# Splitting the next linear's input inside the last chunk of the linear before it, in a 256-token, three-block Trainium2 kernel

## What is computed

```python
for i in range(2):
    xn = rms_norm(h, pre_norm[i])
    out = pool_mixer(xn, ...) if i == 0 else mla_mixer(xn, ...)   # ends in @ w_out
    h = h + rms_norm(out, post_norm[i])
    gate = sigmoid(rms_norm(h, ple_norm[i]) @ ple_w_gate[i])
    h = h + (p[i] @ ple_w_proj[i]) * gate
kv = rms_norm(mem, mem_norm) @ w_ckv            # memory keys and values
h = h + hybrid_mixer(rms_norm(h, norm_mix)) @ w_out
h = h + cross_attention(rms_norm(h, norm_cross) @ w_cq, kv) @ w_co
h = h + (silu(conv(gate)) * val) @ w_down       # val, gate = rms_norm(h, norm_ffn) @ w_up
out = rms_norm(h, norm_final)
```

## Time and profile before

| | |
|---|---|
| median of 3 runs | 2591.68 us (2591.64 to 2591.83) |
| the profiled execution, its own time | 2595.02 us |
| its span in the profile | 2593.2 us |
| PE busy | 2519.5 us, 97% |
| DVE busy | 1540.7 us, 59% |
| ACT busy | 1326.6 us, 51% |
| POOL busy | 83.7 us, 3% |
| mean granted TensorE clock | 0.995 |
| HBM read | 447.25 MB, 173 GB/s over the span |

### The profile page before, as it was taken

The page is one execution under the profiler, slowest core; times in us unless marked ns, Lnnn a source line. Parts: engine busy times, 40 slices in busy tenths (PEclk is TensorE's granted clock), DMA queues, the critical chain, the costliest instruction groups (busy, mean ns, idle before and its releaser), DMA issues. The chain is left out here.

```text
span 2593.2 us, 34914 instructions
## 1 busy us (share of the span) xinstructions
PE 2519.5 (97%) x12890; PEld 2140.7 (83%) x12890; DVE 1540.7 (59%) x1814; ACT 1326.6 (51%) x1747; POOL 83.7 (3%) x124
## 2 busy tenths in 40 slices
PE   8999999999999999999899998899999999999998
PEld 7888888888778898778688887777888888888886
DVE  6665766644655555565555445755666666776554
ACT  5544444544656656464555445435544544554443
POOL 0000000000000000110100002000000000000010
PEclk9999999999999999999999999999999999999999
DMA  8666666555455543565566662054456666656563
GB/s 294 189 188 189 186 188 185 200 194 185 163 162 182 176 132 132 179 228 187 155 181 182 190 190 64 30 165 146 130 172 192 180 193 182 190 171 202 195 199 110
DMA packets 233424, 450.95 MB, mean 174 GB/s; under 512 B 14468, under 2 KB 59728, under 8 KB 232285
## 3 DMA queue, kind: packets, MB, share of 16 engines
q1 hardware_dynamic: 230518, 435.97, 54.2%
q0 software_dynamic: 2624, 13.27, 1.5%
q10 hardware_dynamic: 168, 0.19, 0.0%
HBM read 447.25 MB, written 2.12 MB: 173 GB/s over the span
## 5 line engine op out<-in xcount | busy, mean ns | idle before, releaser
L1598 DVE TENSOR_TENSOR w_lo<-raw,w_hi 128x1024 fp32r<-128x1024 f32 x852 | 1047.2, 1234 | 820.6 <-ACT w_hi L1102 801.6
L1102 ACT ACTIVATE w_hi<-raw 128x1024 fp32r<-128x1024 f32 x852 | 898.9, 1059 | 995.1 <-PE ps L648 637.0
L669 PE MATMUL ps<-x_hi_lo,w_hi 128*128 128x512 f32 x2336 | 822.9, 394 | 13.9 <-DVE w_lo L1598 13.9
L671 PE MATMUL ps<-x_hi_lo,w_lo 128*128 128x256 f32 x2336 | 661.1, 283 | 0.0
L669 PEld LDWEIGHTS ps<-x_hi_lo,w_hi 128*128 128x128 f32 x2336 | 439.4, 188 | 117.0 <-issue 8.7
L646 PE MATMUL ps<-w_hi,x_hi_lo 128*128 128x512 f32 (+3 forms) x1280 | 500.9, 391 | 21.1 <-DVE x_hi_lo L1627 12.4
L648 PE MATMUL ps<-w_hi,x_hi_lo 128*128 128x512 f32 (+3 forms) x1280 | 493.1, 385 | 0.0
L647 PE MATMUL ps<-w_lo,x_hi_lo 128*128 128x512 f32 (+3 forms) x1280 | 491.5, 384 | 0.0
L671 PEld LDWEIGHTS ps<-x_hi_lo,w_lo 128*128 128x128 f32 x2336 | 439.8, 188 | 0.0
L646 PEld LDWEIGHTS ps<-w_hi,x_hi_lo 128*128 128x128 f32 x1280 | 241.5, 189 | 76.3 <-issue 23.8
L648 PEld LDWEIGHTS ps<-w_hi,x_hi_lo 128*128 128x128 f32 x1280 | 241.2, 188 | 43.2
(11 more groups left out here) (316 smaller groups left out, 2200.4 us busy)
## 6 DMA issues: line engine op xcount, KB each, us to landing
raw<-in_w_up SPq DMA_DIRECT2D x160, 512.0 KB, 3.9
raw<-in_pool_w_in SPq DMA_DIRECT2D x128, 512.0 KB, 3.8
raw<-in_w_in SPq DMA_DIRECT2D x96, 480.0 KB, 4.0
raw<-in_w_down SPq DMA_DIRECT2D x76, 512.0 KB, 4.6
raw<-in_pool_w_out SPq DMA_DIRECT2D x64, 512.0 KB, 4.4
raw<-in_ple_w_gate SPq DMA_DIRECT2D x64, 512.0 KB, 4.0
raw<-in_mla_w_in SPq DMA_DIRECT2D x56, 448.0 KB, 3.5
raw<-in_pool_w_group SPq DMA_DIRECT2D x32, 512.0 KB, 4.3
```

What stands on the lines that cost most here:

```text
L669: pe.matmul(bank, w_hi[:, slot, cols], xs[:, k].rearrange("p s n -> p (s n)"), start=k == 0, stop=False, skip_group_check=True)
L671: last = pe.matmul(bank[:, 0:T], w_lo[:, slot, cols], xs[:, k, 0, :], start=False, stop=k == nkt - 1, skip_group_check=True)
L1102: act.activation(w_hi[:, u % RING, :], raw[:, slot, :], ACT.Copy).then_inc(S("w_hi"), 1)
L1598: dve.tensor_tensor(w_lo[:, u % RING, :], raw[:, u % RAW, :], w_hi[:, u % RING, :].bitcast(F32), ALU.subtract)\
```

## The change

The groups of the next linear's input are made earlier. While PE works through a chunk, tiles 2g and 2g+1 of `xh` and `xl` are free once unit g of the linear's last chunk has been used, and the next linear's group g is written there.

- **Six groups in the last chunk.** In the last chunk of `gate0`, of `ckv` and of `out2`, PE transposes group g ahead of unit g+1, for g = 0 to 5; ACT and DVE split it there. In the first chunk of the next linear (`mla_in`, `z`, `cq`) groups 6 and 7 are left, transposed ahead of units 3 and 4. In the last chunk of `gate1`, ACT and DVE make the first six groups of the memory linear, without PE.
- **Two groups in `proj`.** The gate linears get groups 0 and 1 after the third of the four `proj` chunks, and group 2 ahead of their first chunk.
- **`co`.** Its four-tile input moves to tiles 12 to 15; after its chunks 1, 2 and 3 two groups each of the FFN's input are made.
- **Heads.** Groups 0 and 1 of `gm` are transposed in steps 16 and 17, the first unit of `mla_out` stands in step 17 ahead of head 14's output product, and group 2 follows step 18. Groups 3 and 4 are transposed ahead of unit 2, and 5 to 7 ahead of units 3 to 5. The four PSUM banks get new roles for it.
- **Around these.** In an early or late group ACT squares before, no longer after, it splits the next weight unit. The two 2 MB loads of the memory go out on POOL after chunk 0 of `mla_out`, no longer after its last. The product of the relative-position table stands ahead of `ckv`'s second chunk, no longer behind it.

Added functions and the edits that set the order (the same edits on the other engines and at the other linears left out):

```diff
 # PE
-        def first_chunk(src, source_ready=None, width=512, banks_ready=None, run=chunk):
+        def first_chunk(src, source_ready=None, width=512, banks_ready=None, run=chunk, early=0):
-            first = t.n["bank"]
+            first = t.n["bank"] - early
             def ready(k):
                 if k % 2 == 0:
-                    if k // 2 + 3 < KT // 2:
-                        turn(k // 2 + 3)
+                    if early <= k // 2 + 3 < KT // 2:
+                        turn(src, source_ready, k // 2 + 3)
...
-            for g in range(3):
-                turn(g)
+            for g in range(early, 3):
+                turn(src, source_ready, g)
...
+        def early_turns(src, source_ready, n):
+
+            def ready(k):
+                if k % 2 == 0 and 2 <= k <= 2 * n:
+                    turn(src, source_ready, k // 2 - 1)
+            return ready
...
+        def layer_end(n, ready_ple, last):
+            updated = lambda g: pe.wait_ge(S(f"h_post{n}"), g // 2 + 1)
             for c in range(NCH):
                 chunk(ph, pl, 2, ready=ready_ple if c == 0 else None)
...
+                    for g in range(2):
+                        turn(h, updated, g)
+            linear(h, updated, early=2, last=last)
...
+        layer_end(0, ready_ple, early_turns(h, updated0, 6))
+
+        first_chunk(h, updated0, MIN_W, early=6)
...
+        def out_ready(k):
+
+            if k % 2 == 0:
+                for g in (3, 4) if k == 4 else (k // 2 + 2,) if 4 < k < 12 else ():
+                    turn(gm, heads_out, g)
+                n = out_first + k // 2
+                pe.wait_ge(S(f"t_free{n % 4}"), n // 4 + 2)
...
+                if i in (HEADS, HEADS + 1):
+                    turn(gm, heads_out, i - HEADS)
+                if i == HEADS + 1:
+                    next(out_units)
...
 # ACT
+        def group(g, g0=None, src=None, slot=None, features=None):
+
+            if features is None:
+                xpose_hi(xh[:, 2 * g:2 * g + 2, :], 2, None if g0 is None else g0 + 2 * g)
+            else:
+                split_hi(xh, features, g, g0)
+            if src is not None:
+                c, tt = g // 2, g % 2
+                square(src[:, tt, c * 512:(c + 1) * 512], sums[:, slot, tt, c:c + 1])
+
+        def early_groups(n, *args, ready=None, **kw):
+
+            hi(2)
+            for g in range(n):
+                if ready:
+                    ready(g)
+                group(g, *args, **kw)
+                hi(1)
+            hi(6 - n)
...
             for c in range(NCH):
                 read_out(chunk(1), lambda tt: proj[:, tt, c * 512:(c + 1) * 512])
+                if c == 2:
+                    for g in range(2):
+                        group(g, GAIN[f"ple{n}"], h, slot + 1)
             for c in range(NCH):
-                s = first_chunk(GAIN[f"ple{n}"], h, slot + 1) if c == 0 else chunk(8)
+                s = first_chunk(GAIN[f"ple{n}"], h, slot + 1, early=2) if c == 0 else chunk(8) if c < 3 else chunk_with(next_groups)
...
 # DVE
             update(1)
-            for c in range(3):
+            for c in range(2):
                 skip(1)
-
-            first_chunk(GAIN[f"ple{n}"], slot + 1, lambda g: update(g + 2) if g < 2 else None)
+            for g in range(2):
+                group(g, GAIN[f"ple{n}"])
+            skip(1)
+
+            first_chunk(GAIN[f"ple{n}"], slot + 1, lambda g: update(g + 2) if g < 2 else None, early=2)
...
                 if c:
-                    lo(8)
+                    if c == NCH - 1:
+                        early_groups(6, *next_groups)
+                    else:
+                        lo(8)
...
 # POOL
+                if n == 1 and c == 0:
+                    load(memf, a["mem_features"], "mem_in")
+                    load(memt, tokens(a["mem_2"][0]), "mem_in")
```

More of the change, by code:

```diff
@@ L723, in first_chunk, with turn, linear @@
             run(xh, xl, KT, width, ready)
-        def linear(src, source_ready=None, banks_ready=None):
-            first_chunk(src, source_ready, banks_ready=banks_ready)
-            for _ in range(3):
-                chunk(xh, xl, KT)
+        def turn(src, source_ready, g):
+            if source_ready:
+                source_ready(g)
+            to_bank(src, g * 256)
+        def early_turns(src, source_ready, n):
[3 more added lines that the diff above has]
+            return ready
+        def linear(src, source_ready=None, banks_ready=None, early=0, last=None):
+            first_chunk(src, source_ready, banks_ready=banks_ready, early=early)
+            for c in range(3):
+                chunk(xh, xl, KT, ready=last if c == 2 else None)
         def columns(xhi=xh, xlo=xl, nkt=KT, turns=2, ready=None, width=512):
@@ L885, in _ @@
         mla_heads()
-        pe.wait_ge(S("at_done"), 4 + HEADS)
+        turn(gm, heads_out, 2)
+        for _ in out_units:
+            pass
+        for _ in range(NCH - 1):
+            chunk(xh, xl, KT)
         V = {"a": lambda kb, hd: z[:, kb, bass.ds(hd * 64 + Z_VA, 64)],
@@ L971, in _ @@
         pe.matmul(TB(b)[0:A_H, 0:384], reltab, relone, start=True, stop=True).then_inc(S("t_full"), 1)
-        first_chunk(h, lambda g: gated(pe, 1, g // 2 + 1), Z_FIRST[0][1])
+        updated1 = lambda g: gated(pe, 1, g // 2 + 1)
+        chunk(xh, xl, KT, ready=early_turns(h, updated1, 6))
+        first_chunk(h, updated1, Z_FIRST[0][1], early=6)
         chunk(xh, xl, KT, Z_FIRST[1][1])
@@ L1057, in _ @@
         for c in range(NCH):
-            chunk(xh, xl, 4, ready=ready if c == 0 else None)
-        first_chunk(h, lambda g: chunk_out(pe, "co", g // 2), run=feature_pairs)
+            chunk(xh[:, 12:16], xl[:, 12:16], 4, ready=ready if c == 0 else None)
+            if c:
+                for g in (2 * c - 2, 2 * c - 1):
+                    turn(h, lambda g: chunk_out(pe, "co", g // 2), g)
+        first_chunk(h, lambda g: chunk_out(pe, "co", g // 2), run=feature_pairs, early=6)
         banks_read(pe, t)
@@ L1382, in mla_heads @@
         def mla_heads():
+            T_BANK, P_BANK = (TB((t.n["bank"] + b) % 4) for b in (0, 2))
             for i in range(HEADS + 3):
@@ L1505, in _ @@
         first_chunk(between=gla_norm)
-        for c in range(1, NCH):
+        for c in range(1, NCH - 1):
             skip(8)
-        products(act, "out2")
-        read_out(first_chunk(GAIN["cross"], h, 10), lambda tt: cqt[:, tt, :], scale=10)
+        early_groups(6, GAIN["cross"], h, 10)
+        t.add("chunk")
+        read_out(first_chunk(GAIN["cross"], h, 10, early=6), lambda tt: cqt[:, tt, :], scale=10)
         attention([CROSS])
         heads_done(act, "end")
-        xpose_hi(xh, 4)
+        xpose_hi(xh[:, 12:16], 4)
         for c in range(NCH):
             skip(2)
-        products(act, "co")
-        read_out(first_chunk(GAIN["ffn"], h, 11), lambda tt: fgr[:, 2 * tt:2 * tt + 2, :].rearrange("p k n -> p (k n)"))
+            if c:
+                for g in (2 * c - 2, 2 * c - 1):
+                    group(g, GAIN["ffn"], h, 11)
+        read_out(first_chunk(GAIN["ffn"], h, 11, early=6), lambda tt: fgr[:, 2 * tt:2 * tt + 2, :].rearrange("p k n -> p (k n)"))
         def silu_conv(nt):
@@ L2035, in _ @@
             skip(8)
-        layer_end(1, 6, "mla_out")
-        first_chunk(GAIN["mem"], 8, last_gated, memf, "mem_split")
-        skip(8)
+        layer_end(1, 6, "mla_out", GAIN["mem"], memf, "mem_split")
+        first_chunk(GAIN["mem"], 8, last_gated, memf, "mem_split", early=6)
         t.add("bank")
-        first_chunk(GAIN["mix"], 9)
+        early_groups(6, GAIN["mix"])
+        t.add("chunk")
+        first_chunk(GAIN["mix"], 9, early=6)
         skip(8)
```

145 lines of the change are left out of this document (88 added, 57 removed).

## The result

The changed kernel took 2573.2 us, median of four runs (2571.8 to 2576.8), beside 2591.8 for the kernel before (median of four, 2591.6 to 2593.8): a ratio of 0.9926, 95% interval 0.9913 to 0.9938, or 18.5 us less. The forecast was 2565.5 with a range of 2558 to 2572, so the sign was right and the time lies 1.2 us above the range.

What follows compares the result with a forecast made beforehand. TensorE (PE, busy 2519.5 us) was taken to set the time, its losses being what can be won. Gains of 2 x 0.8 + 4.9 + 2.4 + 8.5 + 4.0 + 3.1 + 1.7 = 26.2 took 2591.7 to 2565.5 us, range 2558 to 2572.

Steps and rivals of the forecast that it cites:

- One late turn: First chunks: weight split, low part, then group; PE starts 3.45 us after ACT, against 2.79 a unit.
- Cover in the last chunks: Last chunks: ACT and DVE have room for six early groups, with three units split ahead; costed at nothing.
- the slower rival: Last chunks: ACT and DVE lose their lead, units take 4.3 us against 3.14, 35 us lost; 2601, chance 0.03.
- the rival whose turn follows the groups: Last chunks: early units run at 3.28 us against 3.14, losing 4.2 us; 2569.7, chance 0.17.
- Gates: gate0, gate1: two early groups, but a new 2.2 us wait for h's update; gain 0.8 us each.
- The rival's 3.0 with an update that is not late: gate0, gate1: no new wait, 3.0 us each instead of 0.8, heads 4.0; 2559.5, chance 0.15.
- mla_in, z, cq: First chunks with six groups early: gains of 4.9, 4.0 and 3.1 us, cq's after 0.9 for its read-out.
- Eight groups of transposes at 0.35 us, which the change only moves: Between first and steady chunks: transposes account for 2.8 us, counted as moved and not as loss.
- Heads: Heads' end to mla_out's second chunk: gain 2.4 us, with 1.0 and 4.0 as ends.
- I take that drop as staying: Heads' end: the granted clock's drop to 0.57 stays and falls on unit 0, taking half of 3.4 us off.
- At nothing: Moved memory loads near mla_out and the relative table's product ahead of ckv's second chunk: no cost, 3.5 us of cover.
- Its own time was 3.3 us above the median, which I carry over: Whole kernel: profiled 2595.0 was 3.3 us above the median, so the sum was subtracted from 2591.7.

Runs made afterwards that it cites:

- before_again: The kernel before, unchanged, profiled once more to look for its stretches near half clock: 2591.8 us.
- the pairs: Two early groups' transposes one behind the other in every second unit, against the kernel with earlier update and earlier late groups: 2559.9 us.
- warm_cq: Six unread 256-column products in PE's wait between cq and cross attention, added to the kernel with the norm ahead of cq's last unit: 2558.9 us, ratio 0.9870.
- warm_gate: The changed kernel with sixteen unread 256-column products in PE's wait for the update of h in each gate: 2572.2 us against 2573.0.

## Why the prediction was right and wrong, by its steps

- **The bound, and where the change acts**: right. One late turn was the loss, six early groups removed it, and what remained was one gap ahead of unit 6: 0.91, 0.56, 0.75, 0.54 and 0.50 us where 1.0, 0.7, 0.8, 0.7 and 0.7 stood.
- **Cover in the last chunks** ("I cost this at nothing"): right, since PE has no gap in them, and the slower rival did not come. But two units with a group each stand 3.24 us apart and not 3.14, nearly the 3.28 of the rival whose turn follows the groups. Its number nearly came without its mechanism: the 0.10 is the price of the transposes themselves.
- **Gates**: right, as a new wait of 2.05 us and a net of 0.65 and 0.85. The rival's 3.0 with an update that is not late was too high: the update alone moved ahead makes it 0.65 + 1.05 = 1.7 in gate0. It takes the groups one unit ahead as well, and then it is 4.1.
- **mla_in, z, cq**: the terms that were mis-sized, by 1.1, 1.1 and 1.7. "Eight groups of transposes at 0.35 us, which the change only moves" was too cheap: they cost 0.44, so 3.5 and not 2.8 of each place stays after the change: 0.7 of each miss. For cq the wait for the read-out was put at 0.9 and was 1.78, longer than before by 0.38: another 0.9. About 0.4 in mla_in and z is left that no run prices. Timeline of after, DVE's last low part, the norm behind it, and what waits for that:

```profile
1778.78 1.23 DVE L1684 TENSOR_TENSOR w_lo<-raw,w_hi 128x1024 fp32r<-128x1024 f32 x1 [1.57 <-ACT w_hi L1147]
...
1780.56 0.17 DVE L1757 RECIPROCAL rstd<-root 128x2 f32<-128x2 f32 x1 [0.27 <-ACT root L1233]
...
1780.82 1.27 ACT L1238 ACTIVATE cross_q<-ps,rstd 128x512 f32<-128x512 f32 x2 [0.29 <-DVE rstd L1757]
...
1782.18 0.30 PE L991 MATMUL ps<-identity,cross_q 128*128 128x128 f32 x1 [1.79 <-issue]
```

  With PE faster, the norm behind DVE's low part became what ends last. The run with the norm ahead shows it.
- **Heads**: 2.4 forecast, 3.2 measured: 2.2 of work plus about 1.0 of a stretch that did not come back. That 2.4 is near 2.2 is luck. Without a drop the prediction had 4.0, and the measured place gained 3.2; and "I take that drop as staying" failed, since none of 13 profiles has it. The drop was not the transposes' either: in the profile of before the clock fell at 1028.8, 0.4 us ahead of the sixteen transposes of the earlier trace rows, and before_again ran the same sixteen at 1.00. By the rule of the Trainium skill quoted there ("TensorE: Matmul & The Clock Gate", Part 4), the group of transposes alone would not have held the clock. The change put a unit of products there too, and no run here has the one without the other.
- **At nothing**: right. Gate1's first chunk takes 27.6 us as gate0's does, and PE has no wait at the relative table's product.
- **"Its own time was 3.3 us above the median, which I carry over"**: the step that failed most. The forecast missed by 7.7 us. The sum is 3.0 of that (26.2 for 23.2 between the profiles), the carrying over 4.7: it put the changed kernel's median 3.3 below the level of its profile, and the median is 1.4 above it. The step takes for granted that what one execution had in excess is gone in the ordinary executions of both kernels. The runs show otherwise. Of the excess over before_again 1.65 us is a stretch in the hybrid block, which the changed kernel has in all four profiles, so it is no excess there. The three times of before that I used (2591.6 to 2591.8) were also low ones: in four later series of seven or nine runs its median was 2593.1 to 2593.8, so that 1.4 to 2.1 of the 3.3 was the small sample.
- **What that leaves**: the profile of the changed kernel was a lucky one, without a stretch in either gate. Behind its new waits stands one in gate0 in most profiles and in gate1 in some, 1.5 us each, and its median, 2573, is 1.2 us above that profile. With the 1.2 to 1.9 us by which 2595.0 stands above the later medians of before, this is the way from 23.2 us between profiles to about 20 between medians. If the stretches are as frequent as in the profiles, the gates' net gain of 1.5 is used up in an ordinary execution; that is an estimate, and the run with filled waits moved the median by only 0.7.

The range missed for the same reason: its ends were set by rivals of 4 to 6 us in the turn and the update, and held nothing for the carrying over.

## What to carry to other kernels

Before a sum read from one profile is set against a median, take a second and a third profile of the same kernel, see where the executions differ, and ask of each such place whether the change leaves it as it is. Three times are too few for the base: here they were 1.4 us or more too low. When a wait is moved, follow the order on every engine one step further: here an earlier update and an earlier group gave 2.7 and 5.0 us alone and 12.2 together, and 2.7 of the 4.5 us between are that each uncovered the other. The kernel to keep has both edits, the pairs and the norm ahead of cq's last unit: 2559.5 to 2559.7 us, 34 us less than the kernel before.

## What the runs showed of the hardware

- A wait of PE of about 2 us was followed by 3.4 us at 1.2 GHz in some executions of the same program and not in others: 6 of 7 in gate0, 3 of 7 in gate1, 5 of 11 behind cq, 13 of 18 in out2, and never in these places where the wait was absent (gates: 7 profiles) or filled with products (one profile in each gate, two behind cq). Two waits of 1.7 us had none behind them in any of 18 profiles, and the start of the gated linear attention had one in all 18, behind short products with no wait above 0.8 us. The Trainium skill says, in "TensorE: Matmul & The Clock Gate", Part 1, that the number of slow matmuls at a kernel's start varies from run to run; here the same holds in mid-kernel. Why two gates with equal waits differ stays open, and so does why the stretch behind cq comes in some kernels and not in others with the same wait.
- A group of four transposes between two units costs 0.44 us, of which only 0.35 show ahead of the next matmul. Two groups one behind the other cost twice as much.
- Six f32 products of 256 columns stand in the trace as twelve records over 2.75 us, 0.46 us a product and not the 0.23 of one record (warm_cq). Sixteen fp32r products of 256 columns leave sixteen records over 2.08 us, 0.13 us a product (warm_gate).
